# A hybrid decoder layer on one core: cross-attention's logits placed among the query outputs, its turnings among the values, and the first gathering's wait split in two

## What is computed

```python
q = (x @ w_cq).reshape(b, s, 4, 256)
kv = (mem @ w_ckv).reshape(b, 256, 2, 4, 256)
logits = einsum('bqhd,bkhd->bhqk', q, kv[:, :, 0]) * 256 ** -0.5
p = softmax(logits, axis=-1)
o = einsum('bhqk,bkhd->bqhd', p, kv[:, :, 1]).reshape(b, s, d)
x = layer_norm(ALPHA * x + o @ w_co, ln2_g, ln2_b)
# experts: group-limited top-8 routing, 64 SwiGLU experts of width 256, one shared expert
y = shared(x); for e in range(64): y += gates[:, e] * ((silu(x @ g_e) * (x @ u_e)) @ d_e)
x = layer_norm(ALPHA * x + y, ln3_g, ln3_b)
```

## Time and profile before

| | us |
|---|---|
| median of 3 runs | 996.75 (996.31 to 997.37) |
| the profiled execution, its own time | 997.03 |
| its span, first to last instruction | 995.1 |
| PE busy | 978.4 (98%) |
| DVE busy | 514.3 (52%) |
| ACT busy | 394.7 (40%) |
| query outputs, logits, turnings, values on PE | 431 to 471 |
| output projection, norm, router, shared expert | 471 to 513 |
| first gathering | 513 to 519.6 |
| expert pairs | 519.6 to 984 |

### The profile page before, as it was taken

The page is one execution under the profiler, slowest core; times in us unless marked ns, Lnnn a source line. Parts: engine busy times, 40 slices in busy tenths (PEclk is TensorE's granted clock), DMA queues, the critical chain, the costliest instruction groups (busy, mean ns, idle before and its releaser), DMA issues.

```text
span 995.1 us, 15448 instructions
## 1 busy us (share of the span) xinstructions
PE 978.4 (98%) x6354; PEld 701.2 (70%) x6355; DVE 514.3 (52%) x1019; ACT 394.7 (40%) x709; POOL 53.0 (5%) x54
## 2 busy tenths in 40 slices
PE   8999999999999999999999999999999999999995
PEld 7999999999999999998984444344444444444432
DVE  5988555767689966865675422222223222222224
ACT  6776435556577634455341221121122112211214
POOL 0000102333200000000000000000000000000000
PEclk9999999999999999999999999999999999999998
DMA  8585534333354545658857999999999999999993
GB/s 306 183 308 179 198 138 146 122 124 124 127 191 156 199 172 191 234 211 334 324 230 284 416 420 420 419 420 421 419 420 420 421 417 421 420 420 420 419 420 142
DMA packets 42838, 292.43 MB, mean 294 GB/s; under 512 B 4744, under 2 KB 6928, under 8 KB 8080
## 3 DMA queue, kind: packets, MB, share of 16 engines
q1 hardware_dynamic: 41984, 286.19, 72.7%
q0 software_dynamic: 784, 5.24, 1.4%
HBM read 290.36 MB, written 2.63 MB: 294 GB/s over the span
## 4 chain that ended last, share of the span: by engine, by line
PE 93%; DMA 3%; DVE 2%; SPq 1%; ACT 1%; issue 0%; DVEq 0%; ACTq 0%
PE stream L1596 33%; PE stream L1922 20%; PE stream L1946 10%; PE stream L1621 9%; PE work L1911 5%; DMA place_w<-in_wstream 3%; PE stream L1872 1%; PE stream L1876 1%; PE stream L1874 1%; PE stream L1878 1%; PE stream L1932 1%; SPq L531 1%; PE work L1719 1%; PE work L1695 1%; PE work L1808 1%; PE work L1898 1%
## 5 line engine op out<-in xcount | busy, mean ns | idle before, releaser
L1007 DVE TENSOR_TENSOR w_lo<-raw,w_hi 128x1024 fp32r<-128x1024 f32 x142 | 172.5, 1235 | 55.0 <-ACT w_hi L692 54.9
L1922 PE MATMUL stream<-ring,xg 128*64 128x512 f32 x640 | 197.0, 592 | 1.0 <-DMA place_w<-in_wstream 1.0
L692 ACT ACTIVATE w_hi<-raw 128x1024 fp32r<-128x1024 f32 x142 | 147.2, 1052 | 63.7 <-DMA raw<-in_wdense 47.0
L1596 PE MATMUL stream<-xT_hi,w_hi 128*128 128x256 f32 x560 | 159.4, 285 | 0.0
L1596 PE MATMUL stream<-xT_lo,w_hi 128*128 128x256 f32 x560 | 157.9, 282 | 0.0
L1596 PE MATMUL stream<-xT_hi,w_lo 128*128 128x256 f32 x560 | 157.8, 282 | 0.0
L1922 PEld LDWEIGHTS stream<-ring,xg 128*64 128x64 f32 x640 | 62.5, 137 | 92.0 <-issue 92.0
L1596 PEld LDWEIGHTS stream<-xT_hi,w_hi 128*128 128x128 f32 x560 | 106.1, 190 | 3.7 <-issue 3.1
L1596 PEld LDWEIGHTS stream<-xT_hi,w_lo 128*128 128x128 f32 x560 | 105.9, 189 | 0.0
L1596 PEld LDWEIGHTS stream<-xT_lo,w_hi 128*128 128x128 f32 x560 | 105.6, 189 | 0.0
L1463 DVE TENSOR_TENSOR hh<-h,stream 128x256 f32<-128x256 f32 x32 | 13.5, 421 | 170.3 <-ACT h L935 170.3
(11 more groups left out here) (388 smaller groups left out, 2020.2 us busy)
## 6 DMA issues: line engine op xcount, KB each, us to landing
ring<-in_wstream SPq DMA_DIRECT2D x120, 1024.0 KB, 18.3
raw<-in_wdense SPq DMA_DIRECT2D x73, 1024.0 KB, 4.8
place_e<-in_wstream SPq DMA_DIRECT2D x24, 1024.0 KB, 19.1
place_m<-in_wstream SPq DMA_DIRECT2D x12, 1024.0 KB, 16.5
place_c<-in_wstream SPq DMA_DIRECT2D x12, 1024.0 KB, 18.4
place_w<-in_wstream SPq DMA_DIRECT2D x12, 1024.0 KB, 17.8
place_x<-in_wstream SPq DMA_DIRECT2D x12, 1024.0 KB, 19.9
ln<-in_lnp POOLq DMA_DIRECT2D x3, 1024.0 KB, 6.9
```

Source lines behind the costliest of these rows:

```text
L692: nc.scalar.activation(w_hi[:, q % ROUNDED, :], raw[:, q % 6, :], ACT.Copy).then_inc(w_rounded, 1)
L1007: tt(w_lo[:, q % 6, :], raw[:, q % 6, :], w_hi[:, q % ROUNDED, :].bitcast(F32), ALU.subtract).then_inc(w_rest, 1)
L1596: last = mm(S[n % 4][:, 0:SEQ], w[:, b, :], a[:, kb, :], start=(kb + j == 0), stop=(kb == chunks * KB - 1 and j == len(parts) - 1))
L1922: last = mm(S[2][e * SLOTS:(e + 1) * SLOTS, :], feature_block(buf, kb)[:, col + e * SLOTS:col + (e + 1) * SLOTS], tiles[e][kb // 4][:, kb ...
```

## The change

Three edits. PE: the logits of heads 0, 1 and 2 stand after the query outputs 3, 5 and 7, those of head 3 after the turnings of heads 0 and 1; the turnings of heads 2 and 3 stand among the values. ACT and DVE follow in an order to match: ACT's exponentials of heads 0 and 1 stand behind its copies of the query outputs 5 and 7 and the roundings due there, DVE's maxima and probabilities among the rests of the chunks of `co`. In the first gathering, PE waits for the first one-hot ahead of the matmuls that read it and for the second ahead of those that read that one; the shared expert's first turning stands ahead of both waits. SP's and POOL's streams are unchanged.

```diff
@@ ACT
-            for k in range(KB):
-                leave("cq", k, qcT[:, k, :], scale=(D // MEM_HEADS) ** -0.5)
-            for h in range(MEM_HEADS):
+            def cross_exponentials(h):
                 act.wait_ge(cmax_done, h + 1)
...
-            for h in range(MEM_HEADS):
+            def leave_turned(h):
                 act.wait_ge(cpT_mm, h + 1)
...
-            for h in range(MEM_HEADS):
+            def leave_values(h):
                 act.wait_ge(cav_mm, h + 1)
...
+            for k in range(KB):
+                leave("cq", k, qcT[:, k, :], scale=(D // MEM_HEADS) ** -0.5)
+                if k in (5, 7):
+                    cross_exponentials((k - 5) // 2)
+            leave_turned(0)
+            cross_exponentials(2)
+            leave_turned(1)
+            cross_exponentials(3)
+            leave_values(0)
+            leave_turned(2)
+            leave_values(1)
+            leave_turned(3)
+            leave_values(2)
+            leave_values(3)
@@ DVE
             chunk_rests(out_index("cvb", 3))
-            chunk_rests(out_index("cq", 7))
...
-            for h in range(MEM_HEADS):
+            def cross_maximum(h):
                 ve.wait_ge(clog_mm, h + 1)
...
-                if h:
-                    cross_probabilities(h - 1)
-            cross_probabilities(MEM_HEADS - 1)
+            chunk_rests(out_index("cq", 4))
+            cross_maximum(0)
+            chunk_rests(out_index("cq", 6))
+            cross_probabilities(0)
+            cross_maximum(1)
+            chunk_rests(out_index("cq", 7))
+            cross_probabilities(1)
+            cross_maximum(2)
+            cross_probabilities(2)
+            cross_maximum(3)
+            cross_probabilities(3)
@@ PE
+            for k in range(KB):
+                feature_major("cq", k, x1T_r, ready=(xt_rest, 2) if k == 0 else None)
+                if k in (3, 5, 7):
+                    cross_logits((k - 3) // 2)
+            turn_probabilities(0)
+            turn_probabilities(1)
+            cross_logits(3)
+            cross_values(0)
+            turn_probabilities(2)
+            cross_values(1)
+            turn_probabilities(3)
+            cross_values(2)
+            cross_values(3)
@@ PE, the first gathering
-            def gather(kb, bank, buf):
+            def gather(kb, bank, buf, one_hots=None):
...
+                if one_hots is not None:
+                    pe.wait_ge(onehot_done, one_hots - 1)
...
+                if one_hots is not None:
+                    pe.wait_ge(onehot_done, one_hots)
...
-            pe.wait_ge(onehot_done, 2)
             pe.wait_ge(split_l, 2)
...
-                gather(kb, first_banks[kb], 0)
+                gather(kb, first_banks[kb], 0, one_hots=2 if kb == 0 else None)
```

More of the change, by code:

```diff
@@ L1801, in _, with cross_logits @@
             token_major("cvb", 3, memT_r)
-            for k in range(KB):
-                feature_major("cq", k, x1T_r, ready=(xt_rest, 2) if k == 0 else None)
-            for h in range(MEM_HEADS):
+            def cross_logits(h):
                 pe.wait_ge(act_took, taken_count(out_index("cq", 2 * h + 1)))
@@ L1810, in _, with turn_probabilities @@
                 last.then_inc(clog_mm, 1)
-            for h in range(MEM_HEADS):
+            def turn_probabilities(h):
                 pe.wait_ge(cprob_done, TB * (h + 1))
@@ L1817, in _, with cross_values @@
                 last.then_inc(cpT_mm, 1)
-            for h in range(MEM_HEADS):
+            def cross_values(h):
                 pe.wait_ge(cpT_cp, h + 1)
```

## The result

The changed kernel takes 1001.7 us (998.98 to 1002.17, 7 runs) against 996.75: the ratio is 1.0041, with a 95% interval of 1.0032 to 1.0051, so it is slower by 4.1 us (3.2 to 5.1). The two medians lie further apart, by 4.95 us, still inside that interval. The profiled execution took 1000.61 us, with a span of 998.6; it is the second fastest of the seven.

The account below looks back on a forecast made before the run. PE was taken as the bound, busy 978.4 of 995.1 us. A 3.0 us wait less 0.6 us for the one-hots gave +2.4 us, so 999.2 us from 996.75, range 997.2 to 1001.4; the reordering's 0.15 was not subtracted.

Parts of the forecast that it names:

- the first rival: In PE's new wait before projection output 5 the clock falls to half, costing 1.7 us more: 1000.9 us, chance 0.25.
- SyncE's queue: Third raw tile of the output projection issued 3.46 us later, moving the full queue's tail; fourth raw tile lands at 485.5.
- The gap at 478: Dip in DMA rate, with a second about 0.5 us of transfer, which a later tail would fill, subtracted in part.
- Who waits: Output 5 of the output projection waits for the fourth raw tile; PE loses 3.0 us (2.8 to 3.3).
- The clock: At PE's new wait of some 3 us, the forecast (chance 0.50) kept the granted clock at 1.00, at no cost.
- The reordering itself: In the cross-attention, one 1.4 us wait before turning 1 replaces four summing to 1.6 us: gain 0.15 us.
- One-hots: In the first gathering, waiting for the two one-hots one by one gains 0.6 us (0.5 to 0.63).
- The expert stage at nothing: The expert stage's transfers and end shift with its start, so it costs nothing either way.

Follow-up runs that it names:

- the two kernels with one and two halves moved: Kernel before, with one or both halves of the fifth expert tile issued ahead of the fourth raw tile on SyncE: 1000.42 us (1.0033) and 1003.6 us (1.0067).
- the kernels with the mended queue: Changed kernel with the fourth raw tile issued ahead of the fourth expert tile's halves: 996.26 us; the same without the one-hot edit: 996.52 us.
- the first kernel above: Changed kernel with one move on SyncE, the fourth raw tile issued ahead of the fourth expert tile's two halves: 996.26 us, ratio 0.9992.
- the kernel kept warm: Changed kernel with seven matmuls more on PE, their result unread, ahead of output 5 of the output projection: 999.37 us, ratio 1.0021.

## Why the prediction was right, and where its size was off

The direction and the mechanism were right; the kind of loss that came was the first rival's, with a chance of 0.25, and not the forecast's own.

**SyncE's queue** (right). The third raw tile is issued 26.19 us after the first query output's start where it was 22.74: 3.45 us later, 3.46 forecast. The tail moved by as much: in time from the first query output, ACT's rounding of the fourth raw tile went from 51.26 to 54.80, so 3.5 us and not the 3.2 that I took. The gap at 478 that I half subtracted gave nothing back: it stands where some of the DMA engines had run dry, while the last to finish had not, and a landing is that of the last one. This reading of the gap is argued, not shown; that the shift came out at the upper bound (3.46 us, within 0.1) is measured.

**Who waits** (right). Output 5 of the projection, for 3.1 us (3.0 forecast), and 2.3 and 5.0 us in the two kernels with one and two halves moved: one transfer is 2.3 to 2.7 us of PE.

**The clock** (the step that fell short). The forecast let it stay at 1.00 in a wait of 3 us, because waits of up to 1.0 us left it there. It fell after this wait, and after one of 2.3 us too. It did not fall in the wait, as the rival had it: at 487.5 PE had just resumed, and only in the wait of 5.0 us did it fall before PE resumed. The chances of the two should have been the other way round, since the only row with a longer stretch of little work, had shown it falling soon after PE's work had thinned out. Its price of 1.7 us was right for the profiled execution: the clock was low for 3.4 us there (3.5 forecast), at 1.8 us. With it the rival's time was 1000.9, against 1001.7 measured; the ratio on 996.75 gives 1000.8. Three of the seven runs took 1002.0 to 1002.2 us with a mean granted clock of 0.992, the value of the profile with both halves ahead, in which the clock was low for 6.8 us. They probably lost more to the clock than the profiled one (0.994), but none of them has a trace.

**The reordering itself** (small, and of the wrong sign in this execution). Forecast was a gain of 0.15 us; the profile shows 0.3 lost, since the wait before turning 1 was 1.6 us and not 1.4. In the profiles of the kernels with the mended queue it was 1.2 and 1.4, and with 1.2 (the first kernel above) the stretch took 39.75 us, a gain of 0.12. The prediction speaks of four waits that sum to 1.6 us in the kernel before; its rows and the trace have two, of 1.2 us in all, and the other 0.4 us are matmuls that start again after a wait. DVE's queue is as the prediction had it: the third chunk's rest from 455.54, then the probabilities of head 0, the maximum, the fourth chunk's rest, and head 1 at 459.38. It was no part of the loss, because PE would have waited for the tile all the same. What the step missed is that an order without this wait was there to be had.

**One-hots** (right). 0.6 us at the third matmul in the trace of the edit alone and 0.5 at the first expert pair, 0.5 in the changed kernel.

**The expert stage at nothing** (right). 475.4 us in both.

By the ratio (1000.8) the time lies inside the range, 997.2 to 1001.4; the median of the runs, 1001.7, lies 0.3 us above it. The range reached that far only because it took in the clock's fall. The point, 999.2, fits the kernel kept warm (999.37) and the one run of the changed kernel in which the mean clock stayed at 0.996 (998.98).

## What to carry to other kernels

Moving work ahead of an instruction that releases a transfer delays every transfer queued behind it for as long as the queue stays full, also those whose own condition has long been met: before reordering one engine, walk the issuing engine's queue and ask which late transfer is needed first. Put prefetches with slack behind the one that has none, and then look at the next urgent transfer behind them; here one line of SyncE's stream is worth some 5 us. And price a new wait of PE with the clock's fall on top; in this kernel that added more than half of the 3.1 us wait itself.

## What the runs showed of the hardware that I had not expected

PE's clock fell to the 1.2 GHz level after a wait of 2.3 us, and the matmuls after it lost 1.8 us; after 5.0 us of waiting they lost 2.5. After 2.3 and 3.1 us the fall came only when PE was at work again, 1.4 and 0.1 us later. The Trainium skill's page "TensorE: Matmul & The Clock Gate" (Part 1, "HAM oscillation") warns of longer gaps than the shortest one here; the measured 2.3 us decides.

Seven matmuls that nobody reads, put into the wait, gave back most of what the fall cost in the changed kernel (51 matmuls in 6.20 us instead of 7.74), and the runs spread over 0.5 us where those of the changed kernel spread over 3.2. Work in which PE does nothing useful was thus faster than rest.

Near the start of the kernel before the clock column shows 1.00 (the figure after the five engines) while matmuls of 128x256 f32 add 0.43 us each, half the pace of 0.216 us that the same form has in the logits:

```profile
7.00:8.00 1.00, 1.00 (x3) 0.74 (x3) 0.62 (x1) 0.00 (x0) 0.00 (x0) 1.00 0.92 340
```

I read this as the lower level, which the column misses there; no run tests it. The pace of one form of matmul is the better witness.
